# Where the softmax division stands in a top-k attention: inside the transposing products, or on their result

## The chip, the cores and the metric

The kernel runs on one core of a Trainium2 chip. The metric is the device time of one execution in microseconds. Two kernels are compared on the same chip; a change of about 0.2% is what a measurement of this kernel can tell from none.

## What is computed

One inference step of a hybrid encoder: a prompt of 1024 rows and a sample of 64 rows with 512 cached keys go through one layer. Half of the layer is a recurrence (RG-LRU) and stands outside the change. The other half is sparse attention: an indexer picks top-k keys per query, and eight query heads in two groups attend to them. The reference of that part, cut down:

```python
logits = jnp.einsum('bthgd,btkhd->bthgk', qg, kg) * (HEAD_DIM ** -0.5)
logits = jnp.where(valid, logits, neg)
p = jax.nn.softmax(logits, axis=-1)
o = jnp.einsum('bthgk,btkhd->bthgd', p, vg)
yb = rms_norm(ob.astype(dt), g_b) * jax.nn.silu(zb)
x_out = x + gate * (jnp.concatenate([ya, yb], axis=-1) @ w_out)
```

All is float32. The kernel keeps keys that were not picked out by adding a bias of -1e30 to their logits.

## The kernel before

The program is one block with a hand-written stream of instructions for each engine and semaphores between them. The attention stage is the last but one; the output projection is the last, and its first two steps are mixed into the end of the attention.

**Passes.** The attention goes through 18 passes, `PASSES` (L151): a tile of 128 query rows (`i` 0 to 7) or of the 64 sample rows (`i` = 8) with one group `g` of four heads (`GROUP`), in the order i = 2, 8, 3, 4, 5, 6, 7, 1, 0, each with g = 0 and then 1; passes are counted from 0. A pass has `key_tiles(i)` tiles of up to 128 keys: 3 for i = 2, 5 for the sample, then 4, 5, 6, 7, 8, and 2 and 1 at the end, 82 in all.

**Steps.** `attention_order()` (L174) writes the steps out once, and every engine walks the same list and does its own part of each:

- *head* (one of the four heads of the *next* pass). TensorE makes the logits in three products of split halves (`logits_of`, L1664, by `split3`, L564). VectorE adds the bias and takes the row maximum in one instruction (L2150), then turns the maximum into -max x scale (L2153). ScalarE takes the exponential in place and its row sum (`exponentials`, L1287, instruction L1293). VectorE's `invert` (L2116) makes 1/sum (L2120) and the diagonal matrix `diag_a` or `diag_b` with 1/sum on it (L2122). With the last head of a pass ScalarE and POOL (GpSimd) also split the next queries (`q_hi` L1280, `q_lo` L970) and, in passes 3 to 10, a piece of the output weights (`woa_hi` L1301, `woa_lo` L1012).
- *turn* (one key tile). TensorE turns the four heads' exponentials so that keys lie on partitions, by a product with the diagonal matrix, so that the division comes with it (L1715). The result lies in PSUM bank 4 or 5 in turn; ScalarE copies its high half (`pt_hi`, L1370), VectorE takes the rest (`pt_lo`, L2169).
- *mix* (one key tile). TensorE multiplies the values with it in three products and adds them up in bank 6 or 7 (the second `split3` caller, L1733; in the trace L566 to L568 with `pt_hi` and `v_hi`). The first mix of a pass waits until the pass two before has left its bank.
- *out* (end of a pass). ScalarE squares the result (L1382), VectorE multiplies it with the gate `silu_zb` into `y_b` (L2178), POOL adds the squares of the four heads up (L1019 to L1023), and SyncE sends `y_b` to DRAM. SyncE's queue then loads the next gate and the next queries (`load_zb`, `load_q`), in that order and behind the store.
- *fill*, *take*, *prep*: pieces of the output projection in the last four passes; *prep* splits `y_raw` (`y_hi` on ScalarE L1352, `y_lo` on POOL L998).

One turn is always one ahead of the mix, and the heads of the next pass come one or two per key tile, or four after the first tile of a short pass:

```python
if more or not last:
    steps.append(("turn", x + 1))
...
steps.append(("mix", x))
x += 1
steps += heads[:at_once]
```

So the end of a long pass is: last head, turn, mix, turn, mix, first turn of the next pass, last mix, second turn of the next pass, its first mix, its first head. The functions that the diff touches follow.

## Time and profile before

| | |
|---|---|
| median of 3 runs | 1128.11 us (1127.08 to 1128.51) |
| the profiled execution's own time | 1130.15 us |
| its span in the trace | 1128.3 us |
| attention stage (first turn to the first product after the last fill) | 697.6 to 944.8 us |
| granted TensorE clock, mean | 0.973 of full speed |
| busy share of the span | PE 92%, DVE 77%, ACT 44%, POOL 35% |

PE is TensorE, PEld its weight loads, DVE is VectorE, ACT ScalarE, POOL GpSimd, SP SyncE. In the timeline a row gives start, duration, engine, line, operation, out<-in (for a product: moving operand, then stationary one) and how many instructions were merged; in brackets stands how long the engine idled before, and what it waited for. A product's duration has its drain in it, so products overlap in the records, and one should read starts against starts.

### The profile page before, as it was taken

The numbers are of one execution on the slowest core, as the hardware profiler recorded it, in microseconds if no ns is written. First come the engines' busy times: TensorE is split into PE (matmuls) and PEld (weight loads), VectorE is DVE, ScalarE is ACT, GpSimd is POOL, SyncE is SP. The second block draws the span as 40 slices with busy tenths as digits, with TensorE's granted clock in tenths as the row PEclk, the third lists the DMA queues.
The fourth block names the chain that finished last, engine by engine and source line by source line (L and its number), as shares of the span: only waits on it lengthen the run. The fifth ranks groups of instructions, "written<-read, shape, count | busy, mean of one in ns | idle before, by whom it ended". The sixth has DMA issues, their size and how long they took to land.

```text
span 1128.3 us, 16568 instructions
## 1 busy us (share of the span) xinstructions
PE 1039.0 (92%) x5914; PEld 931.5 (83%) x5914; DVE 864.4 (77%) x1643; ACT 494.7 (44%) x827; POOL 392.2 (35%) x247
## 2 busy tenths in 40 slices
PE   5989888999989998989899996899999999999996
PEld 3679666999989998989899995778878878888873
DVE  1578899999998899999999996677667656444344
ACT  4442565211223676765556324556555534111111
POOL 0223665221112444554545571233331332212120
PEclk9989999999999998989999998999999999999998
DMA  9613010232341022222113632243322336132221
GB/s 298 191 43 80 6 40 1 77 115 77 97 135 47 19 80 80 80 80 74 48 39 97 212 105 71 72 108 94 95 57 66 94 94 232 55 114 94 84 66 56
DMA packets 128281, 100.78 MB, mean 89 GB/s; under 512 B 12177, under 2 KB 119201, under 8 KB 128225
## 3 DMA queue, kind: packets, MB, share of 16 engines
q1 hardware_dynamic: 128224, 100.04, 30.2%
q8 instruction: 34, 0.56, 0.2%
...
## 4 chain that ended last, share of the span: by engine, by line
PE 55%; DVE 25%; issue 14%; ACT 4%; DMA 1%; SPq 1%; POOL 1%; DVEq 0%; ACTq 0%
PE ps L566 15%; PE ps L568 15%; PE ps L567 15%; DVE scores L1994 6%; PE ps L1715 5%; DVE best L1990 4%; DVE y_a L2043 3%; DVE hidden L2038 2%; DVE conv L2016 2%; DVE scores L1954 2%; PE ps L1450 2%; PE ps L1435 1%; DVE mult L2033 1%; DVE mult L2024 1%; DMA x_in<-in_x_prompt 1%
## 5 line engine op out<-in xcount | busy, mean ns | idle before, releaser
L566 PE MATMUL ps<-h_hi,w_hi 128*128 128x364 f32 (+3 forms) x984 | 323.8, 329 | 5.1 <-DVE h_lo L1893 4.1
L567 PE MATMUL ps<-h_lo,w_hi 128*128 128x364 f32 (+3 forms) x984 | 322.8, 328 | 0.0
L568 PE MATMUL ps<-h_hi,w_lo 128*128 128x364 f32 (+3 forms) x984 | 322.5, 328 | 0.0
L888 POOL TENSOR_TENSOR w_lo<-w_raw,w_hi 128x1024 fp32r<-128x1024 f32 (+1 forms) x41 | 107.1, 2613 | 316.9 <-ACT w_hi L1079 316.9
L566 PEld LDWEIGHTS ps<-h_hi,w_hi 128*128 128x128 f32 (+1 forms) x984 | 186.4, 189 | 6.8 <-issue 4.2
L567 PEld LDWEIGHTS ps<-h_lo,w_hi 128*128 128x128 f32 (+1 forms) x984 | 186.5, 190 | 1.2
L568 PEld LDWEIGHTS ps<-h_hi,w_lo 128*128 128x128 f32 (+1 forms) x984 | 186.4, 189 | 0.7
L1994 DVE MATCH_REPLACE8 scores<-best,scores 128x512 f32<-128x512 f32 (+6 forms) x204 | 172.3, 858 | 0.0
L1990 DVE MAX8 best<-scores 128x8 f32<-128x512 f32 (+6 forms) x204 | 162.8, 860 | 1.8
L998 POOL TENSOR_TENSOR y_lo<-y_raw,y_hi 128x1024 fp32r<-128x1024 f32 (+1 forms) x18 | 41.3, 2295 | 142.2 <-ACT y_hi L1352 142.2
L2169 DVE TENSOR_TENSOR pt_lo<-ps,pt_hi 128x512 fp32r<-128x512 f32 (+2 forms) x82 | 53.6, 656 | 45.1 <-ACT pt_hi L1370 44.6
L1095 ACT ACTIVATE stage<-ps 128x364 f32<-128x364 f32 (+3 forms) x66 | 28.7, 461 | 130.7 <-PE ps L568 121.9
L1370 ACT ACTIVATE pt_hi<-ps 128x512 fp32r<-128x512 f32 (+2 forms) x82 | 46.4, 568 | 54.6 <-PE ps L1715 54.5
L970 POOL TENSOR_TENSOR q_lo<-q_raw,q_hi 128x512 fp32r<-128x512 f32 (+1 forms) x18 | 21.9, 1218 | 131.9 <-ACT q_hi L1280 131.9
L2216 DVE SCALAR_TENSOR_TENSOR acc<-ps,rstd,acc 128x1024 f32<-128x1024 f32 (+1 forms) x9 | 11.5, 1283 | 70.8 <-PE ps L568 70.8
L1079 ACT ACTIVATE w_hi<-w_raw 128x1024 fp32r<-128x1024 f32 (+1 forms) x41 | 43.1, 1052 | 49.4 <-PE ps L568 36.7
L1954 DVE SCALAR_TENSOR_TENSOR scores<-relu,iw,scores 128x384 f32<-128x384 f32 (+3 forms) x63 | 58.2, 968 | 3.7 <-ACT relu L1134 3.2
L566 PE MATMUL ps<-woa_hi,y_hi 128*128 128x512 f32 (+1 forms) x144 | 56.5, 392 | 1.6 <-DVE acc L2132 1.6
L566 PE MATMUL ps<-wob_hi,y_hi 128*128 128x512 f32 (+1 forms) x144 | 57.0, 396 | 0.0
L568 PE MATMUL ps<-wob_hi,y_lo 128*128 128x512 f32 (+1 forms) x144 | 56.9, 395 | 0.0
L567 PE MATMUL ps<-wob_lo,y_hi 128*128 128x512 f32 (+1 forms) x144 | 56.8, 395 | 0.0
L567 PE MATMUL ps<-woa_lo,y_hi 128*128 128x512 f32 (+1 forms) x144 | 56.1, 390 | 0.0
...
## 6 DMA issues: line engine op xcount, KB each, us to landing
...
w_mod_raw<-in_w_mod SPq DMA_DIRECT2D x8, 1024.0 KB, 12.1
...
```

Source lines behind the costliest of these rows:

```text
L566: nc.tensor.matmul(out, w_part_hi, x_hi, start=first, stop=False)
L567: nc.tensor.matmul(out, w_part_hi, x_lo, start=False, stop=False)
L568: return nc.tensor.matmul(out, w_part_lo, x_hi, start=False, stop=last)
L888: pool.tensor_tensor(w_lo[:, slot, :, 0:width], w_raw[:, slot, :, 0:width], f32(w_hi[:, slot, :, 0:width]), ALU.subtract).then_inc(w_lo_do ...
L998: pool.tensor_tensor(y_lo[:, e % 2, :, 0:rows_], y_raw[:, e % 2, :, 0:rows_], f32(y_hi[:, e % 2, :, 0:rows_]), ALU.subtract).then_inc(y_lo ...
L1079: nc.scalar.activation(w_hi[:, slot, :, 0:width], w_raw[:, slot, :, 0:width], ACT.Copy).then_inc(w_hi_done, 1)
L1370: nc.scalar.activation(pt_hi[0:kr, n % 2, 0:GROUP * rows_], ps[0:kr, 4 + n % 2, 0:GROUP * rows_], ACT.Copy).then_inc(pt_hi_done, 1)
L1715: x = nc.tensor.matmul(ps[0:kr, 4 + n % 2, rows_ * h:rows_ * (h + 1)], probs_of(u)[0:rows_, P * t:P * t + kr], diag_of(u)[0:rows_, 0:rows_ ...
L1954: x = V.scalar_tensor_tensor(out, relu[0:rows_, v % 3, 0:n], iw[0:rows_, i, h:h + 1], out, ALU.mult, ALU.add)
L1990: V.max(w[i][1], w[i][0]).then_inc(select, 1)
L1994: V.match_replace(w[i][0], w[i][1], w[i][0], TAKEN).then_inc(select, 1)
L2169: V.tensor_tensor(pt_lo[0:kr, n % 2, 0:GROUP * rows_], ps[0:kr, 4 + n % 2, 0:GROUP * rows_], f32(pt_hi[0:kr, n % 2, 0:GROUP * rows_]), ALU ...
```

## The change

1. The turn is now a transpose against the unit matrix `ident` and moves the exponentials as they are. The diagonal matrices are gone.
2. `invert` makes 1/sum for four heads in one instruction per pass instead of one per head.
3. A new step *norm*, once per pass and right behind the pass's last turn: four transposes of the 1/sum column, broadcast over 128 columns, put 1/sum of each query along the free axis of every partition. It takes a place in the alternation of banks 4 and 5 (`SLOTS`, `turn_bank`, `turn_bank_free`). ScalarE copies it to `spread`.
4. At *out* VectorE multiplies the result with `spread` into `o_now`; ScalarE's square now reads `o_now` and waits for it; the gate product into `y_b` is POOL's, ahead of its sums.
5. The maximum is taken as a minimum of logits that the same instruction scales by -`SM_SCALE`, so the small instruction L2153 is gone, and the exponential waits for the logits themselves.

```diff
--- before.py
+++ after.py
@@ -202,6 +205,8 @@
                 fill(FILL_BEFORE.get(a, 0))
             if more or not last:
                 steps.append(("turn", x + 1))
+                if TURNS[x + 1][1] == len(key_tiles(PASSES[TURNS[x + 1][0]][0])) - 1:
+                    steps.append(("norm", TURNS[x + 1][0]))
...
 
 
-TURNS = [(a, t) for a, (i, g) in enumerate(PASSES) for t in range(len(key_tiles(i)))]
+SLOTS = [step for step in attention_order() if step[0] in ("turn", "norm")]
...
-    diag_b = z.take("diag_b", [P, 4, P], F32)
+    spread = z.take("spread", [P, GROUP * P], F32)
...
-    diag_a = z.take("diag_a", [P, 4, P], F32)
+    o_now = z.take("o_now", [P, GROUP * P], F32)
...
                 elif kind == "prep":
                     split_y(n)
                 elif kind == "out":
-                    t0, r = tile_at(PASSES[n][0])
+                    i, g = PASSES[n]
+                    t0, r = tile_at(i)
+                    pool.wait_ge(o_done, n + 1)
+                    pool.wait_ge(zb_in[g], 16 * (n // 2 + 1))
+                    if n >= 1:
+                        pool.wait_ge(yb_out, 16 * n)
+                    pool.tensor_tensor(y_b[:, 0:GROUP * r].rearrange("p (h t) -> p h t", h=GROUP),
+                                       o_now[:, 0:GROUP * r].rearrange("p (h t) -> p h t", h=GROUP),
+                                       silu_zb[:, GROUP * g:GROUP * (g + 1), 0:r], ALU.mult).then_inc(yb_done, 1)
                     pool.wait_ge(o_sq_done, n + 1)
...
-                act.wait_ge(max_neg, n + 1)
-                nc.scalar.activation(w, w, ACT.Exp, bias=small[0:rows_, 1, n % 8:n % 8 + 1], scale=SM_SCALE,
+                act.wait_ge(logits, n + 1)
+                nc.scalar.activation(w, w, ACT.Exp, bias=small[0:rows_, 0, n % 8:n % 8 + 1], scale=-1.0,
                                      accum_out=small[0:rows_, 2, n % 8:n % 8 + 1]).then_inc(exp_done, 1)
...
-                    nc.scalar.activation(pt_hi[0:kr, n % 2, 0:GROUP * rows_], ps[0:kr, 4 + n % 2, 0:GROUP * rows_],
+                    nc.scalar.activation(pt_hi[0:kr, n % 2, 0:GROUP * rows_], ps[0:kr, turn_bank("turn", n), 0:GROUP * rows_],
                                          ACT.Copy).then_inc(pt_hi_done, 1)
...
+                elif kind == "norm":
+                    r = GROUP * tile_at(PASSES[n][0])[1]
+                    act.wait_ge(normed, n + 1)
+                    if n >= 1:
+                        act.wait_ge(o_done, n)
+                    nc.scalar.activation(spread[:, 0:r], ps[:, turn_bank("norm", n), 0:r], ACT.Copy).then_inc(spread_done, 1)
...
                     rows_ = tile_at(PASSES[n][0])[1]
-                    act.wait_ge(mixed, TURNS_UPTO[n])
+                    act.wait_ge(o_done, n + 1)
...
-                    nc.scalar.activation(o_sq[:, 0:GROUP * rows_], ps[:, 6 + n % 2, 0:GROUP * rows_], ACT.Square).then_inc(o_sq_done, 1)
+                    nc.scalar.activation(o_sq[:, 0:GROUP * rows_], o_now[:, 0:GROUP * rows_], ACT.Square).then_inc(o_sq_done, 1)
...
+            def turn_bank_free(kind, n):
+
+                s = SLOTS.index((kind, n))
+                if s >= 2:
+                    was, m = SLOTS[s - 2]
+                    pe.wait_ge(pt_lo_done if was == "turn" else spread_done, m + 1)
...
-                    pe.wait_ge(diag_ready, GROUP * (p_ + 1))
-                    if n >= 2:
-                        pe.wait_ge(pt_lo_done, n - 1)
+                    pe.wait_ge(exp_done, GROUP * (p_ + 1))
+                    turn_bank_free("turn", n)
 
                     for h in range(GROUP):
                         u = GROUP * p_ + h
-                        x = nc.tensor.matmul(ps[0:kr, 4 + n % 2, rows_ * h:rows_ * (h + 1)],
-                                             probs_of(u)[0:rows_, P * t:P * t + kr], diag_of(u)[0:rows_, 0:rows_],
-                                             start=True, stop=True)
+                        x = nc.tensor.transpose(ps[0:kr, turn_bank("turn", n), rows_ * h:rows_ * (h + 1)],
+                                                probs_of(u)[0:rows_, P * t:P * t + kr], ident[0:rows_, 0:rows_])
                     x.then_inc(turned, 1)
+                elif kind == "norm":
+
+                    rows_ = tile_at(PASSES[n][0])[1]
+                    pe.wait_ge(inv_done, n + 1)
+                    turn_bank_free("norm", n)
+                    for h in range(GROUP):
+                        c = (GROUP * n + h) % 8
+                        x = nc.tensor.transpose(ps[:, turn_bank("norm", n), rows_ * h:rows_ * (h + 1)],
+                                                small[0:rows_, 3, c:c + 1].broadcast_to([rows_, P]), ident[0:rows_, 0:rows_])
+                    x.then_inc(normed, 1)
...
-                        pe.wait_ge(yb_done, p_ - 1)
+                        pe.wait_ge(o_done, p_ - 1)
...
-            def invert(u):
-
-                r = tile_at(PASSES[u // GROUP][0])[1]
-                dve.wait_ge(exp_done, u + 1)
-                V.reciprocal(small[0:r, 3, u % 8:u % 8 + 1], small[0:r, 2, u % 8:u % 8 + 1]).then_inc(inv_done, 1)
-                dve.wait_ge(inv_done, u + 1)
-                V.tensor_scalar(diag_of(u)[0:r, 0:r], ident[0:r, 0:r], small[0:r, 3, u % 8:u % 8 + 1], None,
-                                ALU.mult).then_inc(diag_ready, 1)
+            def invert(p_):
+
+                r = tile_at(PASSES[p_][0])[1]
+                c = slice(GROUP * p_ % 8, GROUP * p_ % 8 + GROUP)
+                dve.wait_ge(exp_done, GROUP * (p_ + 1))
+                if p_ >= 2:
+                    dve.wait_ge(normed, p_ - 1)
+                V.reciprocal(small[0:r, 3, c], small[0:r, 2, c]).then_inc(inv_done, 1)
...
-            waiting = []
...
                     V.tensor_tensor_reduce(probs_of(n)[0:rows_, 0:keys], src, bias[0:rows_, bias_at(i):bias_at(i) + keys],
-                                           1.0, NEG, ALU.add, ALU.max, small[0:rows_, 0, c:c + 1]).then_inc(logits, 1)
-                    dve.wait_ge(logits, n + 1)
-                    V.tensor_scalar(small[0:rows_, 1, c:c + 1], small[0:rows_, 0, c:c + 1], -SM_SCALE, None,
-                                    ALU.mult).then_inc(max_neg, 1)
-                    late = False
-                    for u in waiting:
-                        invert(u)
-                    waiting = [n]
+                                           -SM_SCALE, -NEG, ALU.add, ALU.min, small[0:rows_, 0, c:c + 1]).then_inc(logits, 1)
...
-                    if n == 0 or waiting and (waiting[0] // GROUP == p_ or late):
-                        for u in waiting:
-                            invert(u)
-                        waiting = []
-                    late = True
+                    if t == 0:
+                        invert(p_)
                     dve.wait_ge(pt_hi_done, n + 1)
-                    V.tensor_tensor(pt_lo[0:kr, n % 2, 0:GROUP * rows_], ps[0:kr, 4 + n % 2, 0:GROUP * rows_],
+                    V.tensor_tensor(pt_lo[0:kr, n % 2, 0:GROUP * rows_], ps[0:kr, turn_bank("turn", n), 0:GROUP * rows_],
...
-                    dve.wait_ge(o_sq_done, n + 1)
-                    dve.wait_ge(zb_in[g], 16 * (n // 2 + 1))
+                    dve.wait_ge(mixed, TURNS_UPTO[n])
+                    dve.wait_ge(spread_done, n + 1)
                     if n >= 1:
-                        dve.wait_ge(yb_out, 16 * n)
-                    V.tensor_tensor(y_b[:, 0:GROUP * rows_].rearrange("p (h t) -> p h t", h=GROUP),
-                                    ps[:, 6 + n % 2, 0:GROUP * rows_].rearrange("p (h t) -> p h t", h=GROUP),
-                                    silu_zb[:, GROUP * g:GROUP * (g + 1), 0:rows_], ALU.mult).then_inc(yb_done, 1)
+                        dve.wait_ge(o_sq_done, n)
+                        dve.wait_ge(yb_done, n)
+                    V.tensor_tensor(o_now[:, 0:GROUP * rows_], ps[:, 6 + n % 2, 0:GROUP * rows_],
+                                    spread[:, 0:GROUP * rows_], ALU.mult).then_inc(o_done, 1)
...
+def turn_bank(kind, n):
+
+    return 4 + SLOTS.index((kind, n)) % 2
```

The order of ScalarE at the end of pass 10 (tile 6, first group; 896 keys), before. `pt_hi` rows are turns, `o_sq` is out:

```order
L1293 ACTIVATE probs_b,small<-probs_b,small 128x896
L1280 ACTIVATE q_hi<-q_raw 128x512
L1301 ACTIVATE woa_hi<-wo_raw 128x1024
L1370 ACTIVATE pt_hi<-ps 128x512 x2
L1382 ACTIVATE o_sq<-ps 128x512
L1370 ACTIVATE pt_hi<-ps 128x512 x2
```

And the same place with the change:

```order
L1307 ACTIVATE probs_b,small<-probs_b,small 128x896
L1294 ACTIVATE q_hi<-q_raw 128x512
L1315 ACTIVATE woa_hi<-wo_raw 128x1024
L1384 ACTIVATE pt_hi<-ps 128x512
L1394 ACTIVATE spread<-ps 128x512
L1384 ACTIVATE pt_hi<-ps 128x512
L1402 ACTIVATE o_sq<-o_now 128x512
L1384 ACTIVATE pt_hi<-ps 128x512 x2
```

The copy `spread` now comes between the `pt_hi` of the pass's last turn and that of the next pass's first, which ran back to back before.

TensorE at the same place with the change; the row with `small` is the new step norm:

```order
L1738 MATMUL ps<-ident,probs_a 128x128 x4
L572 MATMUL ps<-pt_hi,v_hi 128x512
L573 MATMUL ps<-pt_lo,v_hi 128x512
L574 MATMUL ps<-pt_hi,v_lo 128x512
L1738 MATMUL ps<-ident,probs_a 128x128 x4
L1748 MATMUL ps<-ident,small 128x128 x4
L572 MATMUL ps<-pt_hi,v_hi 128x512
L573 MATMUL ps<-pt_lo,v_hi 128x512
L574 MATMUL ps<-pt_hi,v_lo 128x512
L1738 MATMUL ps<-ident,probs_b 128x128 x4
```

Before, the row with `small` is not there, and the turns read `diag_a` and `diag_b` in place of `ident`.

POOL at the ends of passes 13 and 14, with the change; before, the same rows without the two `y_b`:

```order
L1004 TENSOR_TENSOR y_lo<-y_raw,y_hi 128x1024
L1029 TENSOR_TENSOR y_b<-o_now,silu_zb 128x512
L1033 TENSOR_TENSOR o_sq<-o_sq 128x256
L1035 TENSOR_TENSOR o_sq<-o_sq 128x128
L1037 TENSOR_TENSOR hsq<-hsq,o_sq 128x128
L976 TENSOR_TENSOR q_lo<-q_raw,q_hi 128x512
L1004 TENSOR_TENSOR y_lo<-y_raw,y_hi 128x1024
L1029 TENSOR_TENSOR y_b<-o_now,silu_zb 128x512
```

The product that makes `y_b` moved from VectorE to a place behind POOL's split of `y_raw`.

## Rows read from the trace of the kernel before

**Rows 1.** The page: busy time of each engine, share of the span, instructions.
```profile
PE 1039.0 (92%) x5914; PEld 931.5 (83%) x5914; DVE 864.4 (77%) x1643; ACT 494.7 (44%) x827; POOL 392.2 (35%) x247
```
**Rows 2.** Stretches: length, then PE, PEld, DVE, ACT, POOL busy, clock, DMA, GB/s.
```profile
697.60:944.80 247.20, 229.33 (x1370) 195.56 (x1371) 160.00 (x460) 135.62 (x269) 80.09 (x85) 0.99 0.34 94
826.00:843.00 17.00, 16.01 (x98) 14.10 (x98) 11.70 (x28) 9.55 (x18) 5.89 (x6) 1.00 0.27 77
```
**Rows 3.** Timeline of PE, one key tile with a head (896 keys), then the next.
```profile
833.72 1.05 PE L1715 MATMUL ps<-diag_a,probs_a 128*128 128x128 f32 x8
834.53 0.48 PE L566 MATMUL ps<-pt_hi,v_hi 128*128 128x512 f32 x1
...
835.30 0.39 PE L566 MATMUL ps<-k_hi,q_hi 128*128 128x512 f32 x1
...
836.52 1.05 PE L1715 MATMUL ps<-diag_a,probs_a 128*128 128x128 f32 x8
```
**Rows 4.** Timeline of PE, eight transposes of cached keys against the unit matrix.
```profile
659.63 1.04 PE L1640 MATMUL ps<-ident,cache_k_rows 128*128 128x128 f32 x8
```
**Rows 5.** Timeline, the end of pass 10, all engines.
```profile
836.72 1.09 DVE L2150 CUSTOM_DVE_ANT_0 probs_b<-ps,bias 128x896 f32<-128x896 f32 x1 [0.52 <-PE ps L568]
...
837.61 0.60 ACT L1370 ACTIVATE pt_hi<-ps 128x512 fp32r<-128x512 f32 x1 [1.18 <-PE ps L1715]
...
838.10 1.03 ACT L1293 ACTIVATE probs_b<-probs_b,small 128x896 f32<-128x896 f32 x1
...
839.13 0.62 ACT L1280 ACTIVATE q_hi<-q_raw 128x512 fp32r<-128x512 f32 x1
...
839.65 1.04 ACT L1301 ACTIVATE woa_hi<-wo_raw 128x1024 fp32r<-128x1024 f32 x1
...
840.60 1.07 ACT L1370 ACTIVATE pt_hi<-ps 128x512 fp32r<-128x512 f32 x2
...
841.21 1.29 DVE L2169 TENSOR_TENSOR pt_lo<-ps,pt_hi 128x512 fp32r<-128x512 f32 x2 [1.46 <-ACT pt_hi L1370]
...
841.96 0.50 PE L566 MATMUL ps<-pt_hi,v_hi 128*128 128x512 f32 x1 [0.99 <-DVE pt_lo L2169]
...
842.96 0.60 ACT L1382 ACTIVATE o_sq<-ps 128x512 f32<-128x512 f32 x1 [1.29 <-PE ps L568]
...
843.59 0.69 DVE L2178 TENSOR_TENSOR y_b<-ps,silu_zb 128x512 f32<-128x512 f32 x1 [1.09 <-ACT o_sq L1382]
...
844.34 0.39 PE L566 MATMUL ps<-k_hi,q_hi 128*128 128x512 f32 x1
```
**Rows 6.** Groups by line: names, shapes, count | busy, mean ns | idle before.
```profile
L1715 PE MATMUL ps<-diag_b,probs_b 128*128 128x128 f32 x264 | 35.3, 277 | 4.2 <-DVE diag_b L2122 4.2
L2122 DVE TENSOR_SCALAR diag_b<-ident,small 128x128 f32<-128x128 f32 (+1 forms) x36 | 12.1, 336 | 1.3
L2120 DVE RECIPROCAL small<-small 128x1 f32<-128x1 f32 (+1 forms) x68 | 10.6, 156 | 3.1 <-ACT probs_b L1293 1.1 <-ACT probs_a L1293 0.7 <-ACT probs_c L1293 0.4
L2153 DVE TENSOR_SCALAR small<-small 128x1 f32<-128x1 f32 (+1 forms) x68 | 10.4, 153 | 2.3
```
**Rows 7.** Timeline of POOL at the end of pass 13.
```profile
894.54 2.39 POOL L998 TENSOR_TENSOR y_lo<-y_raw,y_hi 128x1024 fp32r<-128x1024 f32 x1 [3.45 <-ACT y_hi L1352]
```
**Rows 8.** Timeline, the last pass's query load and what waits for it.
```profile
907.04 0.58 SPq L775 DMA_DIRECT2D q_raw<-q_scratch  x1
...
912.12 0.63 ACT L1280 ACTIVATE q_hi<-q_raw 128x512 fp32r<-128x512 f32 x1 [2.46 <-DMA q_raw<-q_scratch]
...
912.83 1.30 POOL L970 TENSOR_TENSOR q_lo<-q_raw,q_hi 128x512 fp32r<-128x512 f32 x1 [4.97 <-ACT q_hi L1280]
```
**Rows 9.** Stretches (columns as in Rows 2): PE working less, then its clock.
```profile
324.00:328.00 4.00, 2.43 (x18) 2.00 (x17) 3.96 (x9) 2.56 (x5) 1.55 (x1) 1.00 0.00 0
328.00:332.00 4.00, 3.69 (x18) 3.46 (x17) 3.96 (x11) 1.26 (x3) 0.82 (x1) 0.66 0.80 222
...
732.00:736.00 4.00, 4.00 (x16) 2.97 (x15) 2.20 (x8) 1.00 (x3) 0.60 (x2) 0.57 0.71 155
```

12 lines of the change are left out of this document (5 added, 7 removed).

## The prediction, made before the changed kernel ran

> **What bounds the kernel now.** I read the page first, then stretches, the order of the chain and the timeline of one pass. TensorE is busy 92% of the span, VectorE 77%, ScalarE 44% [rows 1]. The change touches only the attention stage, 697.6 to 944.8 us, where PE shows 229.3 of 247.2 us busy [rows 2]. A busy share does not say what a PE instruction saved is worth; the timeline does. There are two kinds of place.
>
> *Key tiles with a head.* One tile takes from turn to turn 836.52 - 833.72 = 2.80 us and PE starts each product as the last lets it [rows 3]. Here PE is the bound, and its savings count in full.
>
> *The end of a pass.* After the last head ScalarE has a queue: `pt_hi` at 837.61, the last exponential 838.10, the query split 839.13, the weight split 839.65, and only at 840.60 the `pt_hi` of the last turn; VectorE's `pt_lo` follows at 841.21 and PE's mix at 841.96, after 0.99 us of idling [rows 5]. PE's savings there only make it wait longer.
>
> **What a turn costs.** A turn of four heads is issued as eight instructions: its record is 1.05 us, one alone lasts 0.28 [rows 3, 6], so one follows the other after (1.05 - 0.28)/7 = 0.11, and the turn holds PE 0.89 us. The transposes against the unit matrix elsewhere are one instruction each: eight of them are a record of 1.04 us [rows 4], again 0.11 apart. So a turn of four becomes 0.445, and the saving is 0.445 us. With 82 turns that is 36.4 us of PE work. The 18 norm steps add 18 x 4 x 0.11 = 8.0; their broadcast source I price as any transpose. PE's work falls by 28 us. If PE were the bound throughout, that would be the gain.
>
> **The other edits.** VectorE loses 72 diagonals of 0.31 us, 54 of 72 reciprocals of 0.16 and 72 scalings of 0.15 [rows 6], 41 us in all. It idled in most tiles, so this shortens only the wait from a head's logits to its exponential by 0.2 us and from the last exponential to the next pass's first turn by 0.5. ScalarE gains 18 copies `spread`, priced as the back-to-back `pt_hi` at 0.53 each [rows 5], 9.6 us. `o_now` on VectorE reads PSUM and costs what `y_b` did, 0.69 [rows 5]. The square stands behind it now, and behind the square, on ScalarE, is the `pt_hi` of the next pass's second turn. The gate product on POOL I price by the nearest row, a difference of 128x512 on POOL, 1.30 us [rows 8]; its bounds are the 0.69 of VectorE and 2.39 for double the width [rows 7]. Behind it are its own sums, SyncE's store, the gate load and the query load.
>
> **A long pass, worked out** (pass 10; time from 836.52). Before: `pt_hi` 4.08, `pt_lo` 4.69, last mix but for one 5.44, first head of the next pass 844.34 = 7.82. After: turn to 0.45, mix to 1.15, turn to 1.59. The norm takes the bank of the turn before, so it waits for that `pt_lo`, which follows VectorE's maximum and ends at 2.02: norm 2.08 to 2.52, mix to 3.22. ScalarE: exponential 1.33, queries 2.36, weights 2.88, `pt_hi` 3.83, `spread` 4.36; `pt_lo` ends at 5.15. The next pass's first turn needs the bank and runs from 5.21 to 5.65; last mix 6.35; second turn 6.80; its first mix waits for `pt_hi` 5.85 and `pt_lo` 7.17, and ends at 7.93. So the end of the pass, with four turns at half price in it, **loses 0.1 us**. VectorE then makes `o_now` to 7.86, ScalarE the square to 8.5 and the second `pt_hi` to 9.03, `pt_lo` 9.75, and the second mix starts at 9.80; before, it came at 7.82 + 1.21 (head) + 0.89 (turn) = 9.92. Only the next two turns, with heads between, are saved clean, 0.89. The pass gains 0.12 + 0.89, say **0.9 to 1.0 us** of the 3.1 that its seven turns save on PE.
>
> **The same chain for the others**, each with its own head, maximum and exponential times, gives per pair of passes (g = 0, 1): tile 2: 0 (the first head of pass 1 waits for POOL) and 0.9; sample: 0.3 and 0.3; tile 3: 0.3 and 0.75; tile 4: 0.35 each; tile 5: 1.1 each; tile 6: 0.9 each; tile 7: 0.6 and 1.1 (heads of 256 keys follow, so a cycle of 1.94 us becomes 1.58, bound by turn, `pt_hi`, `pt_lo`, mix). Sum 9.0 us. Least sure are the short ones, where a tenth in each of four exponentials moves the sum.
>
> **The short passes give back.** At the ends of passes 13 and 14 POOL has the split of `y_raw`, 2.39 us [rows 7], and the gate product is queued behind it, where VectorE made it at once. `y_b` comes about 2.4 us later after pass 13 and 4.1 after pass 14. The load of the last queries was issued at 907.04, right behind the store and the gate load, and `q_hi` waited for it until 912.12 [rows 8]: 2.46 us of ScalarE idling that PE covered with pieces of the output projection. With the load 4.1 us later, `q_hi` is at 916.3, `q_lo` ends at 918.2, and the heads of the last pass, ready on PE at 917.2 at the latest, start 2.3 us later than now. I charge **2.3 us**. After that PE has fills and the output projection without a gap; VectorE's and POOL's later work is covered by some 1 to 3 us there, so the tail costs 0 (bound 1).
>
> **Sum.** 9.0 - 2.3 = 6.7 us. Against the profiled execution: 1130.15 - 6.7 = 1123.5. That one lies 2.0 above the median of the three, 1128.11; my forecast is for the median: **1121.5 us**.
>
> **A rule against the change.** Where PE works less the clock can fall: in 324 to 328 it was busy 2.43 of 4 us, with transposes and waits for ScalarE, and in the next 4 us the granted clock was 0.66; at 732 to 736, after tiles of 64 rows, 0.57 [rows 9]. That is TensorE's lower level of 1.2 GHz for some 2.7 to 3.4 us, and costs about half of it. In the long pass above PE would work 4.3 of 7.2 us in the end of the pass, and more than 2 of these are transposes. The Trainium skill ("TensorE: Matmul & The Clock Gate", Part 4: PE-mode transpose) says that transposes do not count as work to the gate, so the high rate is not kept up by them. By that rule the ends of the passes would be mostly idle to the gate, and many would lose the clock; the trace neither shows nor denies it, since its stretches of transposes have idling in them too. This is the third rival.
>
> **The rivals.**
> 1. *PE sets the pace nearly everywhere* and the waits at the ends overlap better than my chain: the gain is between 15 and 28 us, 1100 to 1113. For it: PE's share of 93% in the stage. Against it: 1.46 and 0.99 us of waiting in the end of pass 10 behind a ScalarE that the change loads more. Chance 0.13.
> 2. *The ScalarE queue and the new serial steps win.* `spread` (0.53), the bank wait for norm and the square behind `o_now` (0.7) stand in a chain at 18 ends. If a further 0.4 us shows per pass, 7 us, the gain is gone: 1126 to 1130, no change. Chance 0.13.
> 3. *The clock falls at the ends of passes.* One fall costs up to 1.7 us of PE work, of which some is hidden in waits; at 16 ends with 1.2 each it costs 19 us, and 1128.1 - 6.7 + 19 = 1140. It decides from six ends on, where the gain is used up. For it: the rows above. Against it: whole passes with PE waiting 1 to 1.7 us kept 1.00 [rows 2]. Chance 0.17, with 1129 to 1142.
> 4. *The transposes are not single-pass here*, and a turn costs 0.89 as before: the change would be slower by norm, `spread` and POOL's delay, +5 to +12. Against it: the same form of instruction in rows 4, float32 from SBUF. Chance 0.04.
>
> The forecast as worked out, 1116 to 1125.8, has 0.53.
>
> **How the numbers follow.** Faster by over 0.2% (below 1125.9): 0.53 + 0.13 + 0.01 = 0.67. Slower by over 0.2% (above 1130.4): most of rivals 3 and 4 and a little of 2, 0.20. Within: 0.13. The range for 8 in 10 runs from 1110, which leaves out the better part of rival 1, to 1133, which leaves out the half of rival 3; it takes in 2.39 instead of 1.30 for POOL (1 to 2 us more) and a chain a third off. About 0.2% is what a measurement of this kernel can tell from no change.
>
> **What would show it.** Right: turns of four records 0.11 apart, some 0.6 us long; the head tile at 896 keys 2.36 us; PE's work 28 us less and its idling in the stage some 20 us more; the mix of the last key tile waiting for `pt_lo` about 2 us; the last `q_hi` waiting for its load, and POOL's `y_b` behind `y_lo`. Wrong: a head tile that stays above 2.5 us; granted clock below 0.97 in the long passes (rival 3); ends of passes shorter than 7 us (rival 1); `spread` with nothing waiting behind it.

## The result, and the profile after

The changed kernel takes **1124.93 us** (median of 20 runs, 1121.66 to 1129.62); the kernel before, run beside it, 1129.22 us (median of 20, 1126.63 to 1131.80). The ratio is 0.9968, with a 95% interval of 0.9957 to 0.9979: faster by 2.4 to 4.9 us. The forecast was a gain of 6.7 us, from 1128.1 to 1121.5; the sign is right, the gain of the medians is 4.3 us, 0.64 of it.

The page of the changed kernel, busy time of each engine, to be read against [rows 1]:

```profile
PE 1014.3 (90%) x5658; PEld 898.5 (80%) x5658; DVE 825.5 (74%) x1445; ACT 502.2 (45%) x845; POOL 413.2 (37%) x265
```

The attention stage, which stands before in [rows 2] (length, then PE, PEld, DVE, ACT and POOL busy, clock, DMA share, GB/s):

```profile
695.70:941.00 245.30, 208.54 (x1132) 167.41 (x1132) 122.38 (x273) 142.26 (x287) 101.51 (x103) 0.97 0.34 93
```

PE, VectorE and the loads of weights all lost work; ScalarE and POOL gained it. But PE, busy 93% of the stage before, is busy 85% now: its idling grew by 18.9 us, from 17.9 to 36.8 (some 20 was forecast), and its busy time fell by 20.8, where 28 was forecast. By the mean clocks of the two stretches (0.99 before, 0.97 now) work at the lower clock took some 5 us more than before, an estimate, so most of the missing 7 is the clock.

The next view, the change's own groups (as in [rows 6]: shape and count | busy, mean ns | idle before), shows where most of PE's new idling stands: ahead of the turns and of the norm, above all for `pt_lo`. (The mixes wait for `pt_lo` too, 7.5 us in all, against 4.2 before.)

```profile
L1738 PE MATMUL ps<-ident,probs_a 128*128 128x128 f32 (+2 forms) x152 | 23.1, 277 | 8.0 <-DVE pt_lo L2187 4.1 <-ACT probs_a L1307 1.9 <-ACT spread L1394 1.4
...
L1748 PE MATMUL ps<-ident,small 128*128 128x128 f32 (+1 forms) x72 | 11.5, 285 | 10.8 <-DVE pt_lo L2187 10.8
```

To see where the time went I read from both traces when the first product with the values starts in each pass. Each entry is how much sooner than before it starts, counted from the same product of pass 0 (itself 0.5 us sooner after the stage's first turn):

| pass | 2 | 4 | 6 | 8 | 10 | 12 | 13 | 14 | 15 | 17 |
|---|---|---|---|---|---|---|---|---|---|---|
| gained so far, us | 1.2 | 2.0 | 2.7 | 2.8 | 5.7 | 7.6 | 9.2 | 6.0 | 4.2 | 3.5 |

The passes up to 12 gained 9.2 us; passes 13 and later gave 5.6 of it back. Counted from the stage's first turn to the first product behind it, the stage is 4.05 us shorter (247.43 to 243.38). From there to the end of the span it is 183.3 and 183.2 us: nothing changed. Ahead of the stage, where the two kernels do the same work, these two single executions differ by 1.9 us too (697.60 and 695.69), which the change doesn't explain; the medians' 4.3 us is to be read against the stage's 4.05.

**What gave it back** stands in two timelines of the changed kernel. The queue of SyncE from the store of pass 12's `y_b` to the query load for pass 16 (start, length, instruction):

```profile
870.30 0.38 SPq L819 DMA_DIRECT2D y_scratch<-y_b  x1
870.72 0.51 SPq L793 DMA_DIRECT2D silu_zb<-zb_scratch  x1
871.29 1.18 SPq L802 DMA_DIRECT2D y_raw<-y_scratch  x2
872.51 1.87 SPq L781 DMA_DIRECT2D q_raw<-q_scratch  x1
889.43 0.38 SPq L819 DMA_DIRECT2D y_scratch<-y_b  x1
889.85 0.51 SPq L793 DMA_DIRECT2D silu_zb<-zb_scratch  x1
890.74 0.38 SPq L781 DMA_DIRECT2D q_raw<-q_scratch  x1
```

And what the engines did from there on, `y_b` of pass 12 first and then the end of pass 13 (in brackets the idle time before and what ended it):

```profile
868.99 1.28 POOL L1029 TENSOR_TENSOR y_b<-o_now,silu_zb 128x512 f32<-128x512 f32 x1 [3.79 <-DVE o_now L2197]
...
878.90 0.63 ACT L1294 ACTIVATE q_hi<-q_raw 128x512 fp32r<-128x512 f32 x1 [2.01 <-DMA q_raw<-q_scratch]
...
879.44 1.07 ACT L1384 ACTIVATE pt_hi<-ps 128x512 fp32r<-128x512 f32 x2
...
880.05 1.29 DVE L2187 TENSOR_TENSOR pt_lo<-ps,pt_hi 128x512 fp32r<-128x512 f32 x2 [2.92 <-ACT pt_hi L1384]
...
880.88 1.09 PE L1748 MATMUL ps<-ident,small 128*128 128x128 f32 x4 [2.30 <-DVE pt_lo L2187]
...
885.76 2.39 POOL L1004 TENSOR_TENSOR y_lo<-y_raw,y_hi 128x1024 fp32r<-128x1024 f32 x1 [4.89 <-ACT y_hi L1366]
...
888.11 1.29 POOL L1029 TENSOR_TENSOR y_b<-o_now,silu_zb 128x512 f32<-128x512 f32 x1
...
895.55 0.63 ACT L1294 ACTIVATE q_hi<-q_raw 128x512 fp32r<-128x512 f32 x1 [5.00 <-DMA q_raw<-q_scratch]
...
897.54 1.01 PE L1748 MATMUL ps<-ident,small 128*128 128x128 f32 x4 [3.77 <-DVE pt_lo L2187]
...
907.91 0.63 ACT L1294 ACTIVATE q_hi<-q_raw 128x512 fp32r<-128x512 f32 x1 [5.10 <-DMA q_raw<-q_scratch]
```

From the store of `y_b` of pass 12 to the queries of pass 15 in SBUF is a chain of 878.90 - 870.30 = 8.60 us: store, gate load, two loads of `y_raw`, query load. ScalarE would have been free for them 6.6 us after the store. In the kernel before the same chain had 8.49 us, and `q_hi` started without a wait, 6.28 us after the issue of its load; the trace gives 6.3 us from this issue to the landing, so it started just as the load landed:

```profile
880.62 0.38 SPq L813 DMA_DIRECT2D y_scratch<-y_b  x1
...
882.83 1.72 SPq L775 DMA_DIRECT2D q_raw<-q_scratch  x1
...
889.11 0.63 ACT L1280 ACTIVATE q_hi<-q_raw 128x512 fp32r<-128x512 f32 x1
...
900.66 0.63 ACT L1280 ACTIVATE q_hi<-q_raw 128x512 fp32r<-128x512 f32 x1 [0.32 <-DMA q_raw<-q_scratch]
```

So the slack of that load was already nil before. `q_hi` stands ahead of the pass's last `pt_hi` in ScalarE's queue, `pt_lo` waits for that, and the norm and the next turn wait for `pt_lo`. Around these waits the granted clock falls, and PE works off the next pieces slowly (the four transposes at 880.88 take 1.09 us where 0.60 is usual; clock before DMA share and GB/s, as above):

```profile
880.00:884.00 4.00, 3.12 (x12) 2.75 (x13) 1.37 (x3) 1.10 (x3) 0.87 (x1) 0.57 0.00 0
896.00:900.00 4.00, 2.46 (x10) 2.20 (x10) 1.98 (x3) 3.22 (x6) 3.58 (x2) 0.70 0.00 0
```

### The profile page after: what moved, and what is told of

Its sections match the earlier page's. It is cut to its first block, busy times and chain, and to the rows that moved or that the text cites. A ratio compares the mean times of both kernels' runs of the same rounds, so it can differ in the third digit from the quotient of the medians.

```text
span 1122.3 us, 15980 instructions
## 1 busy us (share of the span) xinstructions
PE 1014.3 (90%) x5658; PEld 898.5 (80%) x5658; DVE 825.5 (74%) x1445; ACT 502.2 (45%) x845; POOL 413.2 (37%) x265
## 4 chain that ended last, share of the span: by engine, by line
PE 50%; DVE 24%; issue 15%; ACT 5%; DMA 2%; SPq 1%; POOL 1%; DVEq 1%; ACTq 0%; POOLq 0%
PE ps L572 15%; PE ps L573 14%; PE ps L574 14%; DVE scores L2026 6%; DVE best L2022 5%; DVE y_a L2075 3%; DVE hidden L2070 2%; DVE conv L2048 2%; PE ps L1470 2%; PE ps L1738 1%; DVE scores L1986 1%; DMA q_raw<-q_scratch 1%; PE ps L1455 1%; ACT pt_hi L1384 1%; DVE mult L2065 1%
## 5 line engine op out<-in xcount | busy, mean ns | idle before, releaser
L574 PE MATMUL ps<-woa_hi,y_lo 128*128 128x512 f32 (+1 forms) x144 | 56.2, 390 | 0.0
```

Source lines behind the costliest of these rows:

```text
L574: return nc.tensor.matmul(out, w_part_lo, x_hi, start=False, stop=last)
```

## The experiments

The theories. **A**: the give-back is the query loads, which stand in SyncE's queue behind a store that now comes later. **B**: it is the added links themselves: `spread` and the square on ScalarE, and the bank that the norm takes out of the turns' alternation. **C**: it is the clock. Line numbers in an experiment's rows are its own, some lines off those of the changed kernel. The load at 872.51 is that for pass 15, the one at 890.74 that for pass 16; the expectation of experiment 4 numbers them one lower. The median of the kernel before was between 1128.2 and 1128.7 us in these comparisons; times below are medians. An experiment's interval reaches 1.5 to 2.7 us to either side, so a difference of under about 3 us between two experiments is not told by their medians alone.

### 1. Query loads one pass earlier (q_early)

```diff
             load_zb(1)
+            load_q(2)
             for p_, (i, g) in enumerate(PASSES):
...
-                if p_ + 2 < len(PASSES):
-                    load_q(p_ + 2)
+                if p_ + 3 < len(PASSES):
+                    load_q(p_ + 3)
```

> The changed kernel with each load of queries (L781) one pass earlier in SP's queue: load_q(p+3) ahead of the wait for y_b of pass p, where load_q(p+2) stood; load_q(2) stands ahead of the loop. Nothing else moves. Theory A (the gain of the long passes is given back in passes 13 to 15 because the loads of queries stand behind the store of a y_b that is now late on POOL): the waits of q_hi for DMA, 12.8 us on four instructions in the changed kernel, fall to under 1.5 us, the norms of passes 13 and 14 no longer wait 2.3 and 3.8 us for pt_lo, the first mixes of passes 14 to 17 come 3 to 5 us earlier, and the time falls by 2.5 to 5 us against the changed kernel, to about 1121. Theory B (the loss of those passes is ScalarE's added copies and the bank that the norm takes out of the turns' alternation; the loads only end last there): the q_hi waits vanish too, but others take their place and the time falls by less than 1 us. Theory C (the clock falls at the ends of passes): the granted clock at 880:884 and 896:900 stays under 0.75, less than 1 us gained.

Measured: **1119.21 us**, ratio to before 0.9914 [0.9898, 0.9930]; 5.7 us less than the changed kernel. The queries of passes 15 to 17 are there when ScalarE comes to them, three rows without a bracket:

```profile
880.65 0.62 ACT L1295 ACTIVATE q_hi<-q_raw 128x512 fp32r<-128x512 f32 x1
...
890.93 0.61 ACT L1295 ACTIVATE q_hi<-q_raw 128x512 fp32r<-128x512 f32 x1
...
897.77 0.62 ACT L1295 ACTIVATE q_hi<-q_raw 128x512 fp32r<-128x512 f32 x1
```

Counted as in the table above, the gain grows on from 6.7 us at pass 13 to 9.9 at pass 17. The three stretches of the stage, up to the first product of pass 5, to that of pass 13, and to the end, first in the kernel before, then changed, then here:

```profile
697.60:755.01 57.41, 51.30 (x321) 41.22 (x321) 37.29 (x126) 33.21 (x74) 18.61 (x22) 0.97 0.34 93
755.01:880.04 125.03, 117.58 (x721) 102.82 (x721) 87.01 (x217) 74.58 (x134) 38.39 (x40) 1.00 0.29 81
880.04:945.03 64.99, 60.69 (x332) 51.72 (x332) 35.92 (x119) 28.06 (x61) 23.08 (x25) 1.00 0.42 120
```
```profile
695.69:750.53 54.84, 45.00 (x252) 33.60 (x253) 27.75 (x71) 33.41 (x78) 22.60 (x26) 0.91 0.35 97
750.53:868.46 117.93, 100.61 (x560) 81.52 (x561) 69.58 (x129) 78.88 (x142) 48.24 (x47) 1.00 0.31 85
868.46:939.07 70.61, 61.01 (x302) 50.39 (x303) 23.12 (x69) 28.83 (x65) 30.66 (x31) 0.95 0.36 95
```
```profile
697.06:753.44 56.38, 46.47 (x252) 34.72 (x253) 27.90 (x71) 33.47 (x78) 22.53 (x26) 0.88 0.37 99
753.44:872.32 118.88, 102.10 (x560) 82.82 (x561) 69.97 (x129) 78.84 (x142) 48.18 (x47) 0.99 0.31 85
872.32:934.05 61.73, 57.96 (x302) 47.63 (x303) 23.19 (x69) 28.96 (x65) 30.67 (x31) 1.00 0.39 103
```

The last stretch, 65.0 us before, is 70.6 after the change and 61.7 here, with the clock back at 1.00; passes 13 to 16 show no fall here and in experiment 3. Late loads don't always bring one: experiment 12 has late loads and no fall there. In that stretch alone the profiles differ by 8.9 us, more than the 5.7 of the medians: 1.5 and 1.0 us are lost again in the stretches before it, where the clock fell more often here, and 1.4 ahead of the stage, where nothing was changed. What is left of the change's gain in the early passes, 2.6 us, is 1.0 here, with the clock at 0.88 in place of 0.91.

### 2. The same edit on the kernel before (before_q_early)

> The same edit of SP's queue on the kernel before. There q_hi waited 3.8 us for loads in all (2.46 us the largest). Theory A: it gains 1 to 2.5 us, clearly less than the same edit gives the changed kernel, since y_b left VectorE early there. If the edit gives both kernels the same (within 0.7 us), the give-back in the changed kernel is not made of these loads. Theory B and C: within 1 us of the kernel before.

Measured: 1129.55 us, ratio 1.0012 [0.9990, 1.0034]. Nothing, less than the 1 us that A allowed at the least: the 2.46 us that the last `q_hi` waited [rows 8] were all covered. In the profiles no pass's first product moves by as much as 0.1 us. The loads cost nothing before the change and 5.7 us after it; the change made them late.

### 3. Only the last four loads early (last_loads_early)

```diff
-                if p_ + 2 < len(PASSES):
-                    load_q(p_ + 2)
+                if p_ < 12:
+                    load_q(p_ + 2)
+                if 11 <= p_ and p_ + 3 < len(PASSES):
+                    load_q(p_ + 3)
```

> The changed kernel with only the last four loads of queries early (from pass 14 on); the loads of passes 2 to 13 stay where they stood. Theory A says that all of the 5.7 us of q_early is in the short passes 13 to 17: 1119 to 1120 us. If early loads in the long passes contributed (or cost, as the lower clock of q_early's early passes could mean): above 1121 or below 1118.

Measured: **1118.53 us**, ratio 0.9904 [0.9882, 0.9926], 6.4 us less than the changed kernel, and as good as experiment 1. What the loads cost lay with the last four.

### 4. POOL's order (yb_first)

On POOL, each of `("prep", 0)` and `("prep", 1)`, the two splits `y_lo`, is taken from its place and put behind the next `("out", ...)`, so that `y_b` of passes 13 and 14 goes first.

> The changed kernel with POOL's y_b product and sums of passes 13 and 14 ahead of the y_lo split (L1007) behind which they stood in the changed kernel; SP's queue as in the changed kernel. Theory A with POOL's order as the cause of the late y_b: y_b of pass 13 ends about 2.3 us earlier, the load of queries for pass 15 (890.74 in the changed kernel) is issued 2.0 to 2.5 us earlier, and the time falls by 1.5 to 2.5 us. If what makes y_b late is only that a product on POOL takes 1.3 us after o_now, or if the query load of pass 14 (issued 872.5, before any y_lo) is what starts the loss, the gain is under 1 us. Theory B: 0 +- 0.5 us.

Measured: 1124.56 us, 0.4 less than the changed kernel: nothing that can be told. The loads did come earlier (`q_hi` of passes 15 to 17 waited 7.1 us in all and not 12.1), but another wait took their place. PE now stood for `y_lo`, ahead of the first piece of the output projection:

```profile
892.50 0.80 PE L572 MATMUL ps<-woa_hi,y_hi 128*128 128x512 f32 x1 [2.24 <-POOL y_lo L1004]
```

The queue of POOL behind `y_lo`, which the forecast took for the cause of the give-back, is real, but turning it round pays nothing. The clock has a part in this: it was 0.50 at 892 to 896 and 0.68 at 896 to 900 in this profile; the changed kernel had 1.00 and 0.70 there.

### 5. What the turns alone are worth (two_pass_turns)

A *two-pass* turn is one that is issued as eight instructions, as before the change ([rows 3], `x8`); a *single-pass* one is four.

```diff
-                        x = nc.tensor.transpose(ps[0:kr, ...], probs_of(u)[...], ident[0:rows_, 0:rows_])
+                        x = nc.tensor.matmul(ps[0:kr, ...], probs_of(u)[...], ident[0:rows_, 0:rows_],
+                                             start=True, stop=True)
```

> The changed kernel with its 82 turns as fp32 products with the identity instead of transposes (two passes through the array each, as with the diagonal in the kernel before); the norm, spread, o_now, the one instruction for maximum and scale and everything else stay. It prices the single-pass turns alone. By the forecast's steps a turn is 0.445 us longer, and long passes are longer by 0.9 to 1.1 us where the PE bounds a pass's end: the time rises by 5 to 8 us, to above the kernel before (1130 to 1133). If the ends of the passes are bound by ScalarE and the serial steps (the forecast's second rival), PE has room and the time rises by under 2 us. If PE bounds nearly all of the stage: 15 us or more.

Measured: **1143.92 us**, ratio to before 1.0142 [1.0118, 1.0166]; 19.0 us more than the changed kernel. Of the 36.4 us of PE work in the second passes of 82 turns, a good half was on the path. That is far more than the 5 to 8 us that the expectation drew from the forecast's steps, and in the range that it gave to PE bounding nearly all of the stage: the forecast's chain of pass 10 has the net right, but taken by themselves its cheaper turns were worth more than twice what was put down to them. It also says what the rest of the change costs, with its late loads (`q_hi` of the last three passes waited 12.6 us for them here): 15.2 us over the kernel before, for a norm that is only 8 us of PE work. The change is the difference of two large numbers.

### 6. The maximum's part alone (merge_alone)

The kernel before, with the reduction scaled by `-SM_SCALE` and kept as a minimum, the exponential reading that column with scale -1, and the small scaling between them gone.

> The kernel before with only the maximum's part of the change: the reduction scales by -SM_SCALE and keeps the minimum, the exponential reads that column, and the small DVE instruction of 0.11 us between the two (L2153) is gone; the diagonals and the two-pass turns stay. The rows of before show ScalarE waiting 33 us in all for that small instruction on 24 exponentials. Theory: only the serial step of 0.11 us and its semaphore hop go, at places where PE, with its two-pass turns, is what is waited for; between no gain and 1.5 us. If it gains 3 us or more, part of what the forecast put down to the turns belongs to this edit.

Measured: 1130.21 us, ratio 1.0018 [1.0003, 1.0033]. No gain. The 33 us that ScalarE waited for the small instruction were slack. The profiled execution, 1126.33 us, is the shortest of its twelve, and the clock's fall of [rows 9] at 732 is missing in it:

```profile
732.00:736.00 4.00, 4.00 (x24) 3.01 (x23) 3.14 (x11) 2.08 (x6) 0.00 (x0) 1.00 0.65 159
```

Pass 3, in which that fall stands, takes 10.81 us here and 12.48 in the kernel before; passes 2 and 4 beside it differ by 0.06 us at most. So one fall cost some 1.7 us there.

### 7. The norm out of the turns' banks (norm_bank)

On top of q_early, the norms of passes 0 to 13 go to the accumulation bank that is free between the neighbouring passes, and the turns alternate by themselves.

```diff
-SLOTS = [step for step in attention_order() if step[0] in ("turn", "norm")]
+SLOTS = [step for step in attention_order() if step[0] == "turn" or step[0] == "norm" and step[1] >= SMALL_PASS]
...
+    if kind == "norm" and n < SMALL_PASS:
+        return 7 - n % 2
     return 4 + SLOTS.index((kind, n)) % 2
...
+                    if t == 0 and 1 <= p_ <= SMALL_PASS:
+                        pe.wait_ge(spread_done, p_)
```

> q_early (the changed kernel with loads of queries one pass earlier, 1119.2 us) with the norms of passes 0 to 13 written to the accumulation bank that stands free between the neighbouring passes (7 - n % 2), so that the turns alternate between banks 4 and 5 by themselves; the order of instructions is the same. Theory B1 (the norm's slot in the turns' alternation costs at each pass's end): its waits for pt_lo (4.8 us on 9 products) and those of turns for pt_lo and spread (9.2 and 3.0 us) fall by more than half, and 2 to 5 us are gained. Theory B2 (the norm costs its own PE and ScalarE time, not its bank): within 1 us of q_early.

Measured: **1110.08 us**, ratio 0.9836 [0.9813, 0.9858]: 9.1 us less than q_early, more than B1 said. In the profiles the stage is 7.3 us shorter (236.99 to 229.65) and another 2.4 lie ahead of it (697.06 and 694.62), where the two kernels do the same, so some of the 9.1 may be scatter. The end of pass 10 shows why, first changed, then norm_bank. From the last turn of pass 10 to the first head of the next pass:

```profile
828.21 0.60 PE L1738 MATMUL ps<-ident,probs_a 128*128 128x128 f32 x4
...
829.18 0.62 PE L1748 MATMUL ps<-ident,small 128*128 128x128 f32 x4 [0.37 <-DVE pt_lo L2187]
...
832.36 0.63 PE L1738 MATMUL ps<-ident,probs_b 128*128 128x128 f32 x4 [1.86 <-DVE pt_lo L2187]
...
835.26 0.40 PE L572 MATMUL ps<-k_hi,q_hi 128*128 128x512 f32 x1
```
```profile
825.36 0.60 PE L1743 MATMUL ps<-ident,probs_a 128*128 128x128 f32 x4
...
825.79 0.60 PE L1753 MATMUL ps<-ident,small 128*128 128x128 f32 x4
...
827.04 0.60 PE L1743 MATMUL ps<-ident,probs_b 128*128 128x128 f32 x4
...
829.42 0.50 PE L572 MATMUL ps<-pt_hi,v_hi 128*128 128x512 f32 x1 [1.79 <-DVE pt_lo L2194]
...
831.36 0.39 PE L572 MATMUL ps<-k_hi,q_hi 128*128 128x512 f32 x1
```

With the norm in the alternation, the next pass's first turn must wait until `pt_lo` has read the bank of the last turn (832.36, after 1.86 us). Without it, that turn runs before the wait (827.04), its `pt_hi` follows in ScalarE's queue at once (829.02), and the stretch from the last turn to the next head falls from 7.05 to 6.00 us. Against q_early passes 10 and 11 are 1.05 us shorter each, passes 5 and 9 by next to nothing. The norm had cost the order one turn of lookahead; its work was the small part.

### 8. The norm done twice (norm_twice)

norm_bank with the norm's loop over heads run twice over.

> norm_bank with each norm's four transposes done twice over (same place, same result): 72 more single-pass products of 0.11 us, 8 us of PE. Where PE bounds a pass's end this costs its full length: plus 6 to 8 us. If the ends are bound by ScalarE and the chain behind the last turn: plus 2 to 4 us. If heads cover it: under 1 us.

Measured: **1109.97 us**, the same as norm_bank's 1110.08, for eight microseconds more of PE work. At the ends of the long passes that work is free: from the turn of pass 10's last head tile to the next pass's first head it takes 7.13 us in both (822.17 to 829.30 here, 824.23 to 831.36 there), and PE's wait for `pt_lo` is 0.33 shorter:

```profile
823.75 1.04 PE L1753 MATMUL ps<-ident,small 128*128 128x128 f32 x8
...
827.37 0.50 PE L572 MATMUL ps<-pt_hi,v_hi 128*128 128x512 f32 x1 [1.46 <-DVE pt_lo L2194]
```

Passes 5, 6 and 9 to 12 differ by at most 0.03 us. In passes 13 and 15, which hold two norms each, it is not free: they take 0.87 and 0.90 us longer, the full length of the added work, with PE over 90% busy already. Pass 13, norm_bank and then norm_twice:

```profile
863.11:876.69 13.58, 12.39 (x76) 10.23 (x77) 7.97 (x19) 9.21 (x20) 4.38 (x6) 1.00 0.51 136
```
```profile
861.01:875.46 14.45, 13.16 (x85) 11.07 (x85) 8.04 (x19) 9.65 (x21) 4.84 (x6) 1.00 0.51 128
```

What makes up for these 1.8 us in the profiles is the clock, 0.99 over the stage against 0.97 in norm_bank. So the equal times are in part luck, and the finding is for the long passes.

### 9. The norm earlier in the pass (norm_bank_mid)

norm_bank with the norm behind the turn of tile `max(2, k/2)` of `k`, in place of the last.

> norm_bank with the norms (and the copies to spread on ScalarE) of the long passes moved from ahead of the last tile's products to behind the turn of the middle tile (tile max(2, k/2) of k). If the ends of passes are bound by serial steps and ScalarE's queue (the forecast's second rival), taking 0.58 us of copy and 0.44 us of PE from there gains another 2 to 5 us over 13 passes. If PE bounds them, the moved 0.44 us costs the same where it stands now: within 1 us of norm_bank.

Measured: 1112.55 us, ratio 0.9866 [0.9843, 0.9889]: 2.5 us **slower** than norm_bank, with intervals that overlap a little. In the profiles 0.9 us of it build up in small steps by the first product of pass 11, and 2.0 come in pass 11, behind a fall of the clock at that pass's start which norm_bank does not have:

```profile
828.00:832.00 4.00, 2.22 (x14) 1.70 (x13) 2.03 (x4) 2.03 (x4) 3.61 (x2) 0.97 0.00 0
832.00:836.00 4.00, 4.00 (x15) 3.14 (x14) 1.30 (x3) 1.27 (x3) 2.90 (x4) 0.61 0.39 102
```

Where the norm's 0.44 us of PE and 0.58 of ScalarE stand among tiles with heads they seem to cost a little; at the end of a long pass, by experiment 8, the PE part costs nothing, so nothing could be won by clearing it. Whether the fall comes of the move isn't settled: experiment 10's profile has one at the same place, without this move.

### 10. The square behind the next copy (square_late)

ScalarE's list is changed so that each `("out", a)` stands behind the next `("turn", ...)`; on q_early.

> q_early with ScalarE's Square of o_now (L1403) moved behind the next turn's pt_hi copy in passes 0 to 15. In the changed kernel it waits 18.2 us on 16 passes for o_now, with pt_hi of the next turn queued behind it. If ScalarE's wait there is on the path of the ends: 2 to 4 us gained (PE waits for pt_lo fall). If it is hidden by heads: 0 +- 1 us. A loss would come from sums that POOL gets later and, behind them, q_lo or y_b of the next pass.

Measured: 1115.99 us, ratio 0.9884 [0.9863, 0.9905], 3.2 us less than q_early, about as much as the two intervals allow one to tell. The profiles agree: the stage is 3.65 us shorter, 1.45 of it in passes 13 and 14 with the clock at 1.00 in both. The wait for `o_now` in front of the next pass's second `pt_hi` was on the path.

### 11. Both (bank_square)

> norm_bank (loads of queries early, norms out of the turns' alternation, 1110.1 us) with ScalarE's Square moved behind the next turn's pt_hi copy. Alone on q_early that move gave 3.2 us. If it saves a wait of its own at the ends of passes (norm_bank still waits 19.7 us for o_now ahead of the Square, and PE 32 us for pt_lo): 2.5 to 4.5 us more, 1106 to 1107.5. If it only made up for the turn that the norm's slot took from the lookahead: within 1 us of norm_bank.

Measured: **1103.43 us**, ratio 0.9782 [0.9767, 0.9797], the fastest of the series: 6.7 us less than norm_bank, more than the 3.2 alone; part may be the clock, which in the profiles fell once here, at 696 to 704, and at four places in norm_bank. ScalarE's waits for `o_now` ahead of the square, 19.7 us in norm_bank, are 5.4 here. Its stage has the same work as the changed kernel's in 222.65 us (243.38 there); its first stretch takes 50.28 us with the clock at 0.97, where the changed kernel had 54.84 at 0.91.

### 12. The bank with the loads late (bank_late_loads)

> norm_bank without the early loads: the changed kernel with the norms of passes 0 to 13 in the accumulation banks and SP's queue as in the changed kernel. If the bank's 9.1 us and the loads' 5.7 us are separate sums: 1124.9 - 9.1 = 1115.8 us. If a faster end of pass leaves the loads still less time, so that they eat part of it (theory A carried on): 1117 to 1121 us, with q_hi waiting over 13 us for DMA.

Measured: 1119.13 us, ratio 0.9926 [0.9904, 0.9948]. The bank gives 5.8 us here, 9.1 with early loads, so by the medians late loads take 9.0 us from the kernel with the bank and 5.7 from the one without. That faster passes make them dearer isn't shown by it: the intervals reach 2.5 us to either side, `q_hi` of the last three passes waits 12.7 us for DMA here and 12.1 in the changed kernel, and in the profiles the last stretch loses less to the loads here (7.0 us against 8.9).

### 13. Two-pass turns with the norm out of the way (two_pass_bank)

> norm_bank with two-pass turns (products with the identity). It leaves of the change only that 1/sum is applied behind the products with the values, with every cost of the norm's place taken away. The forecast took a turn's second pass as 0.445 us of PE, 36.4 us in 82 turns, of which the removal would be worth 0.9 to 1.1 us at each pass's end. The price of the second pass in the changed kernel was 19.0 us. If that price stands here too: 1129 us, the time of the kernel before, so all of the gain is the turns'. If the gain of norm_bank was lookahead for ScalarE and VectorE that two-pass turns hide: 1131 to 1136. If moving 1/sum frees VectorE in a way that pays by itself: under 1126.

Measured: 1131.31 us, ratio to before 1.0022 [1.0007, 1.0036]. Without its transposes, and with the norm well placed and the loads early, the change is worth nothing, or a loss of 0.8 to 4.1 us: 1/sum behind the products costs at least what the diagonals cost. Its first products fall 3.6 us behind those of the kernel before in pass 2, with the clock at 0.60 in 720 to 724 there, and from then to pass 17 the distance stays between 3.3 and 4.8 us. The single-pass turns are worth 21.2 us here.

### 14. Busier early passes (slow_turns_first)

q_early with the two-pass product of experiment 5 for `p_ < 6`, to keep PE busy where the clock fell.

> q_early with the turns of passes 0 to 5 (23 of 82) as two-pass products, as in two_pass_turns, and those of the later passes as transposes. They keep PE busier where it idled and where the granted clock fell in q_early (0.88 over passes 0 to 4, against 0.97 in the kernel before). Priced as in the forecast, 23 turns give back 0.445 us each, 10 us, of which by the 19 us that 82 cost in two_pass_turns 5 to 6 us would show. If the clock's falls are what the early passes lost (theory C): the falls go, the granted clock of the stretch rises to 0.95 or more, and the time rises by under 2.5 us or falls. If the falls cost little: plus 4 to 6 us.

Measured: 1125.60 us, ratio 0.9966 [0.9952, 0.9981], 6.4 us more than q_early, what 23 turns should give back by their price in experiment 5 and a little over. The test failed in its aim: the clock did not stay up, it fell for longer in the passes of 64 rows, with PE busy 20.15 of 22 us:

```profile
728.00:750.00 22.00, 20.15 (x100) 16.57 (x99) 6.91 (x20) 9.17 (x24) 6.78 (x8) 0.66 0.13 31
```

It says nothing on what a fall costs; it only shows that more work in these passes is no remedy.

## Why the prediction was right in sign and short in size

**The turn: right.** Four instructions in a record of 0.60 us, 0.11 apart, and the head tile of 896 keys takes 2.36 us, as forecast:

```profile
824.72 0.60 PE L1738 MATMUL ps<-ident,probs_a 128*128 128x128 f32 x4
...
827.08 0.60 PE L1738 MATMUL ps<-ident,probs_a 128*128 128x128 f32 x4
```

Rival 4 is out.

**The end of pass 10: right in its links, 0.25 us short.** The first head of the next pass starts 8.18 us after the last head tile's turn (827.08 to 835.26), forecast 7.93, before 7.82. Each link is there: the norm waits for `pt_lo`, the next turn 1.86 us for the next `pt_lo` (the forecast's sign put these 2 us on the mix behind it, which doesn't wait), the square 1.35 us for `o_now`. `spread` took 0.58 there (0.53 forecast), `o_now` 0.68 (0.69), `y_b` on POOL 1.30 (1.30).

**The long passes: right in sum, in part by luck.** Forecast 9.0 us for passes 0 to 13, 7.9 without the last of them; measured 9.2 for passes 0 to 12. By pairs it was less even: 1.2, 0.8, 0.7, 0.1, 2.9, 1.9 us for pairs 0 to 5, where 0.9, 0.6, 1.05, 0.7, 2.2 and 1.8 were forecast, and pass 12 gave 1.6 where 0.6 was. The clock fell three times in the first five passes (0.62, 0.70 and 0.65 in 700 to 704, 728 to 732 and 736 to 740), once before [rows 9]. At 1.3 to 1.7 us for one fall (rival 3, below) that took some 3 us, an estimate; with the clock of before the sum would have come out near 12.

**The step that failed: "The short passes give back ... I charge 2.3 us".** The forecast followed one load, that of the last queries, and took POOL's `y_lo` for what delays it. That delay came about as forecast: counted from the next pass's first product, the store of `y_b` is 2.1 us later after pass 13 and 3.0 after pass 14 (2.4 and 4.1 forecast). It was not what the time hung on (experiment 4). Pass 13 was to gain 1.1 us and lost 3.2; that miss of 4.3 is more than the whole difference between 6.7 and 4.05. With the loads early pass 13 takes 14.14 us, against 17.53 in the changed kernel and 14.35 before: 3.4 of the 4.3 are the load's, and 0.9 the chain's, which had promised 1.1 and gives 0.2. From pass 14 to 17 the loss was 2.4, close to the 2.3, but by luck: it came of two late loads, with a clock fall behind the first (896 to 900), and with the loads early the same passes *gain* 3.0 us, for which the forecast had no term. What was left out is the slack: the trace of the kernel before shows at 900.66 a `q_hi` with 0.32 us of wait and at 889.11 one without, with its load issued only 6.3 us ahead. Passes that end earlier, behind a store that `o_now` and POOL's slower product make 1.3 us later against the pass's first product, leave those loads short; how much is the earlier end and how much the later store no run separates. It took a wait of 2 us in pass 13, ahead of everything that the end of the pass hangs on. Experiments 1 to 3 show it: 5.7 to 6.4 us, all in the last loads, none before the change. With the loads in time the change gains 1128.5 - 1118.5 = 10.0 us.

**A slip in a sum.** VectorE's savings add up to 42 us by the prediction's own factors, and not 41; the page shows 38.9 (864.4 to 825.5). Nothing hung on it.

**Rival 1** (PE sets the pace nearly everywhere) is out as a whole: the time is not in its range, and the work that experiment 8 adds at the ends of the long passes is free. Away from these ends it holds, in the tiles with heads (experiment 5) and in passes 13 and 15 (experiment 8). Its range, 1100 to 1113, was reached only with the loads, the bank and the square out of the way (1103.4).

**Rival 2** (ScalarE's queue and the new serial steps): right in its mechanisms, which was more than the forecast gave it. They were worth 9.1 us (the bank) and 3.2 us (the square) each on top of the early loads, 15.8 together; but they were already in the forecast's chain of pass 10, so the sum held.

**Rival 3** (the clock at the ends of passes): partly. The forecast said that a granted clock under 0.97 in the long passes would speak for it; it is 1.00 over the 117.9 us from pass 5 to pass 12, with PE busy 100.6 of them. By the rule of the Trainium skill that was weighed there ("TensorE: Matmul & The Clock Gate", Part 4: PE-mode transpose), transposes do not count as work to the gate; here the ends of eight passes, made of transposes, waits and the mixes between them, lost no clock, so the trace bears out nothing of it for them. But the first five passes did lose, 0.91 against 0.97, and in other variants of the kernel a fall does stand at the end of a long pass (experiments 9 and 10). Two readings give the price of a fall. One is pass 3 of experiment 6, 1.7 us. The other is pass 4, which takes 12.09 us in q_early with the clock at 0.50 and 0.82 in its middle, and 10.76 in the changed kernel, where those stretches show 0.92 and 1.00: some 1.3 us for one fall. The stage of the changed kernel shows five falls and that of the kernel before one, so by these prices the clock took some 5 to 7 us in all, an estimate: about 3 in the early passes, and the rest at 880 and 896, around the waits for the late loads. What brings on the early ones stays open.

Among the expectations the largest misses were five: the turns alone are worth 19.0 us where 5 to 8 were expected; the square on top of the bank gave 6.7 where 2.5 to 4.5 were; early loads gave the kernel before nothing where 1 to 2.5 us were expected; the norm's bank gave 9.1 where 2 to 5 were; and moving the norm to mid-pass lost 2.5 where it should have gained or stayed.
